# Attention queries turned in fp32, two heads at a time, with their high and low parts made from the turned bank

## What is computed

```python
aq = rope(aq.reshape(B, S, ATT_HEADS, ATT_HEAD_DIM), positions)   # 16 heads of 64
ak = rope(ak.reshape(B, S, ATT_KV_HEADS, ATT_HEAD_DIM), positions)  # 4 key heads
...
scores = jnp.einsum('bnqhgd,bnkhd->bnhgqk', qb, kk) * (hd ** -0.5)  # blocks of 128, window of two blocks
scores = jnp.where(mask, scores, -jnp.inf)
mx = jnp.maximum(scores.max(axis=-1, keepdims=True), sink)
p = jnp.exp(scores - mx)
probs = p / (p.sum(axis=-1, keepdims=True) + jnp.exp(sink - mx))
out = jnp.einsum('bnhgqk,bnkhd->bnqhgd', probs, vv)
```

## Time and profile before

| | us |
|---|---|
| median of 3 runs | 1392.05 (1391.99 to 1392.17) |
| the profiled execution | 1391.64 |
| its span, first to last instruction | 1389.9 |
| PE busy | 1328.2 (96%) |
| DVE busy | 668.1 (48%) |
| ACT busy | 397.0 (29%) |
| POOL busy | 662.6 (48%) |
| turning `q_parts` on PE, L607, x128 | 21.0 |
| `q_high` on ACT, L852, x32 | 417 to 422 ns each |

### The profile page before, as it was taken

One profiled execution on the slowest core, in us unless ns is written; L12 is line 12 of the kernel. 1 busy time (PEld: TensorE's weight loads), 2 busy tenths in 40 slices (PEclk: granted clock), 3 DMA queues, 4 the chain that ended last, 5 costly groups with the idle time before them and its releaser, 6 DMA issues.

```text
span 1389.9 us, 20009 instructions
## 1 busy us (share of the span) xinstructions
PE 1328.2 (96%) x6846; PEld 1128.8 (81%) x6846; DVE 668.1 (48%) x1297; ACT 397.0 (29%) x926; POOL 662.6 (48%) x854
## 2 busy tenths in 40 slices
PE   3499999999999999999999999999999999999997
PEld 2398797989877888889978987898789888688886
DVE  5979886785873000153265235424542321544335
ACT  5334445353450100023322332333132311311111
POOL 6834507061366544295267146715661455557340
PEclk9799999999999999999999999999999999999999
DMA  9411102010021220230131031103210132321502
GB/s 350 123 45 31 47 2 61 15 32 28 0 61 61 75 79 26 89 93 17 48 89 30 0 90 46 30 0 92 59 30 15 45 92 91 106 91 61 197 16 106
DMA packets 119832, 89.30 MB, mean 64 GB/s; under 512 B 13305, under 2 KB 111721, under 8 KB 118894
## 3 DMA queue, kind: packets, MB, share of 16 engines
q1 hardware_dynamic: 116288, 76.16, 17.9%
q10 hardware_dynamic: 3502, 12.61, 2.6%
HBM read 80.35 MB, written 8.41 MB: 64 GB/s over the span
## 4 chain that ended last, share of the span: by engine, by line
PE 82%; DVE 12%; issue 2%; ACT 2%; DVEq 0%; ACTq 0%
PE pp L532 24%; PE pp L533 23%; PE pp L534 23%; PE pp L718 2%; PE pp L728 2%; PE pp L638 1%; DVE y_lo L1294 1%; DVE prob L1237 1%; DVE num L1404 1%; PE pp L710 1%; PE pp L621 1%; PE pp L629 1%; PE pp L723 1%; PE pp L622 1%; PE pp L607 1%
## 5 line engine op out<-in xcount | busy, mean ns | idle before, releaser
L484 POOL TENSOR_TENSOR w_hi<-raw,ones 128x256 fp32r<-128x256 f32 x404 | 284.1, 734 | 619.1 <-ACTq L346 341.0
L532 PE MATMUL pp<-h_hi,w_hi 128*128 128x512 f32 x912 | 361.5, 396 | 9.9 <-DVE h_lo L1120 8.3
L533 PE MATMUL pp<-h_lo,w_hi 128*128 128x512 f32 x912 | 356.1, 390 | 0.0
L534 PE MATMUL pp<-h_hi,w_lo 128*128 128x512 f32 x912 | 355.9, 390 | 0.0
L488 POOL TENSOR_TENSOR w_lo<-raw,w_hi 128x256 fp32r<-128x256 f32 x404 | 345.7, 887 | 7.9
L532 PEld LDWEIGHTS pp<-h_hi,w_hi 128*128 128x128 f32 x912 | 171.8, 188 | 49.6 <-issue 6.8
L534 PEld LDWEIGHTS pp<-h_hi,w_lo 128*128 128x128 f32 x912 | 171.8, 188 | 36.0
L533 PEld LDWEIGHTS pp<-h_lo,w_hi 128*128 128x128 f32 x912 | 171.9, 188 | 34.6
L532 PE MATMUL pp<-w_hi,h_hi 128*128 128x384 f32 (+1 forms) x512 | 162.1, 317 | 0.6 <-DVE roped L1214 0.6
L534 PE MATMUL pp<-w_hi,h_lo 128*128 128x384 f32 (+1 forms) x512 | 158.1, 309 | 0.0
L533 PE MATMUL pp<-w_lo,h_hi 128*128 128x384 f32 (+1 forms) x512 | 158.0, 309 | 0.0
(11 more groups left out here) (216 smaller groups left out, 1855.9 us busy)
## 6 DMA issues: line engine op xcount, KB each, us to landing
raw<-w_in SPq DMA_DIRECT2D x72, 512.0 KB, 3.6
w_mod<-w_ada SPq DMA_DIRECT2D x7, 1024.0 KB, 11.5
x_in<-x SPq DMA_DIRECT2D x4, 1024.0 KB, 8.0
raw<-w_att SPq DMA_DIRECT2D x8, 512.0 KB, 5.0
merged_dram<-mix_a ACTq DMA_DIRECT2D x8, 512.0 KB, 2.6
w_gate<-w_ada ACTq DMA_DIRECT2D x8, 512.0 KB, 3.4
raw<-w_m SPq DMA_DIRECT2D x8, 512.0 KB, 3.6
mix_in<-merged_dram ACTq DMA_DIRECT2D x8, 512.0 KB, 3.3
```

The source lines that it names most:

```text
L484: ins = pool.tensor_tensor(hi[:, q, :], raw[:, s, q, :], one[:, q, :], ALU.mult)
L532: pe.matmul(o, lh, rh, start=first, stop=False)
L533: pe.matmul(o, lh, rl, start=False, stop=False)
L534: return pe.matmul(o, ll, rh, start=False, stop=last)
```

## The change

The two heads of a pair are turned together, in fp32, straight out of `roped`: a transpose of 128 tokens by 2 x 64. In bank 2 the even head of the pair then stands on partitions 0 to 63 and the odd one on 64 to 127. `copy_qk` copies each half to the same half of `q_t` as fp32r, the high part; `q_low` subtracts it from the bank and writes the low part to the other half of `q_t`. So the even heads have high above low and the odd ones low above high, which is the same to `scores`. `q_high`, `q_parts` and `ident_r` go. `q_low` moves from block u-2 to block u-3, ahead of `k_low`, and waits for `copy_qk`; `turn_q` waits until `q_low` of the block before has read the bank; `scores` waits for `q_low`.

```diff
             def turn_q(i, m):
-                after(pe, q_lo_ready, NB * i + m + 1)
                 after(pe, qk_copied, 2 * (NB * i + m))
-                for g in range(4):
-                    ins = pe.matmul(bank(2)[:, g * P:(g + 1) * P], q_parts[:, m % 2, g, :, :], ident_r[:, :], start=True, stop=True)
+                after(pe, q_lo_ready, NB * i + m)
+                for pair in range(2):
+                    ins = pe.transpose(bank(2)[:, pair * P:(pair + 1) * P], roped[:, m % 2, 2 * pair:2 * pair + 2, :, :], ident[:, :])
                 ins.then_inc(qk_turned, 1)
             def scores(i, m):
                 after(pe, qk_copied, 2 * (NB * i + m + 1))
                 after(pe, k_lo_ready, NB * i + m + 1)
+                after(pe, q_lo_ready, NB * i + m + 1)
...
-            def q_high(i, m):
-                after(act, rope_done, 2 * (NB * i + m + 1))
-                if m >= 2:
-                    after(act, qk_turned, NB * i + m - 1)
-                act.activation(q_parts[:, m % 2, :, 0, :], roped[:, m % 2, 0:4, :, :].rearrange("p h a d -> p h (a d)"), ACT.Copy).then_inc(q_hi_ready, 1)
             def copy_qk(i, m):
                 after(act, qk_turned, NB * i + m + 1)
                 after(act, scores_full, NB * i + m)
-                act.activation(q_t[:, :, :], bank(2).rearrange("p (g t) -> p g t", g=4), ACT.Copy).then_inc(qk_copied, 1)
+                for odd in range(2):
+                    r = slice(odd * HD, (odd + 1) * HD)
+                    ins = act.activation(q_t[r, odd:4:2, :], bank(2)[r, 0:2 * P].rearrange("p (g t) -> p g t", g=2), ACT.Copy)
+                ins.then_inc(qk_copied, 1)
...
             def q_low(i, m):
-                after(dve, q_hi_ready, NB * i + m + 1)
-                dve.tensor_tensor(q_parts[:, m % 2, :, 1, :], roped[:, m % 2, 0:4, :, :].rearrange("p h a d -> p h (a d)"),
-                                  q_parts[:, m % 2, :, 0, :].bitcast(F32), ALU.subtract).then_inc(q_lo_ready, 1)
+                after(dve, qk_copied, 2 * (NB * i + m + 1))
+                for odd in range(2):
+                    r, other = slice(odd * HD, (odd + 1) * HD), slice((1 - odd) * HD, (2 - odd) * HD)
+                    ins = dve.tensor_tensor(q_t[other, odd:4:2, :], bank(2)[r, 0:2 * P].rearrange("p (g t) -> p g t", g=2),
+                                            q_t[r, odd:4:2, :].bitcast(F32), ALU.subtract)
+                ins.then_inc(q_lo_ready, 1)
```

More of the change, by code:

```diff
@@ L204, in build @@
         roped = place("roped", [P, 2, 6, 2, 32], F32, X + 7168)
-        ident_r = place("ident_r", [P, P], F32R, X + 10240)
         rot_c = place("rot_c", [P, 10, 32], F32, X + 11264)
         rot_s = place("rot_s", [P, 10, 32], F32, X + 12544)
-        q_parts = place("q_parts", [P, 2, 4, 2, HD], F32R, SCR)
         q_t = place("q_t", [P, 4, P], F32R, SCR + 4096)
@@ L284, in build @@
         x_mod_act, x_mod_dve, h_hi_ready, h_lo_ready = sem("x_mod_act"), sem("x_mod_dve"), sem("h_hi_ready"), sem("h_lo_ready")
-        gates_full, gates_out, ident_r_ready = sem("gates_full"), sem("gates_out"), sem("ident_r_ready")
+        gates_full, gates_out = sem("gates_full"), sem("gates_out")
         row_step, row_act, rows_turned, cols_step = sem("row_step"), sem("row_act"), sem("rows_turned"), sem("cols_step")
@@ L290, in build @@
         rope_product, rope_done, v_copied = counter("rope_product"), counter("rope_done"), counter("v_copied")
-        q_hi_ready, q_lo_ready = counter("q_hi_ready"), counter("q_lo_ready")
+        q_lo_ready = counter("q_lo_ready")
         qk_turned, qk_copied, k_lo_ready = counter("qk_turned"), counter("qk_copied"), counter("k_lo_ready")
@@ L659, in attend @@
                         pe.wait_ge(gates_out, 4)
-                        pe.wait_ge(ident_r_ready, 1)
                     if 2 <= u <= NB + 1:
@@ L824, in _ @@
             act.wait_ge(h_lo_ready, KT)
-            act.activation(ident_r[:, :], ident[:, :], ACT.Copy).then_inc(ident_r_ready, 1)
             def gate_row_step(n):
@@ L882, in attend @@
                         exponentials(i, u - 4)
-                    if 1 <= u <= NB:
-                        q_high(i, u - 1)
                     if 9 <= u <= 12:
@@ L1257, in attend @@
                     if 3 <= u <= NB + 2:
+                        q_low(i, u - 3)
                         k_low(i, u - 3)
@@ L1260, in attend @@
                         split_window(i, u - 5)
-                    if 2 <= u <= NB + 1:
-                        q_low(i, u - 2)
                     if 4 <= u <= NB + 3:
```

## The result

| | before | after |
|---|---|---|
| median, us | 1392.11 (12 runs, 1391.73 to 1393.79) | 1395.79 (12 runs, 1394.31 to 1396.84) |
| profiled execution, us | 1391.64 | 1396.05 |
| its span, us | 1389.9 | 1394.3 |
| PE waits for `prob_t` | 2.0 us, 2 times | 5.8 us, 14 times |
| PE waits for `prob` | 1.8 us, 7 times | 3.3 us, 12 times |

The changed kernel is slower: ratio 1.0024, 95% interval 1.0016 to 1.0032. The forecast was 1396.9, with slower the likeliest. The sign and most of the total are as forecast; how the total is spread over the heads is not, so that the total is near in part by luck.

A forecast was written before the change was run, and what follows sets the result against it. PE was taken to bound the kernel, with 82% of the chain against DVE's 12%. Three heads +4.05, the first +1.5 and a single -0.75 gave +4.8 us on 1391.64; predicted median 1396.9, range 1390.5 to 1400.

The forecast's parts named there:

- PE's gain per block: On PE, six fp32 turnings replace eight: 0.20 us gained in each of 32 blocks, 6.4 if nobody waits.
- DVE's distance: On DVE, start of `sink_d` to start of `prob_t`: 1.27 us instead of 0.28, so `prob_t` comes 0.99 later.
- my case: On DVE, alternating halves hold both `q_low` operations and `k_lo`; `prob_t` 0.99 later, +4.8 us, 1396.9; chance 0.60.
- A: Rival: DVE's neighbours overlap despite alternating halves; `prob_t` 0.66 later, -0.9 us in all, 1391.1; chance 0.25.
- The new waits: In units 6 and 7 of a head, PE waits 0.22 us for `prob_t` and keeps 0.20: nothing gained.
- The table load's cover: On ACT, heads 2 to 4: 1.28 us move to the first `copy_qk`; `k_lo` of block 0 has 0.4 left.
- The chained steps 8 and 9: Units 8 and 9 of a head, bounded by DVE: two at 0.63 add 1.26 us, from 0.6 ahead to 0.7 behind.
- Step 10: Unit 10 of a head, where `q_low` is new: 0.99 us more on DVE, 0.27 and 0.10 absorbed, +0.62.
- The first head: Longer chain with gate rows on DVE and ACT's two copies in the way: -0.6 + 0.15 + 1.26 + 0.72 = +1.5 us.
- The second head: Besides the +1.35 us of each later head, PE's waits at unit 3 and for turning queries go once: -0.75.
- Rival B: DVE's additions hide entirely, as it is busy only 59 of 81 us: -6.4 - 0.75, 1384.9; chance 0.06.
- Rival C: On DVE, the `q_low` halves cost 0.6 us each start to start: 1.5 a head, 6 in all, 1403; chance 0.09.

The follow-up runs named there:

- one-sided run: The changed kernel with both `q_low` operations on partitions 0 to 63 from block 1 of each head, odd low parts left out: 1394.79 us.
- early rows: Gate rows' product and scan moved from step 9 to steps 2 and 3 of the first head: changed kernel 1390.65 us, kernel before 1388.95.
- PE's part alone: The kernel before with queries turned by two fp32 transposes of `roped` instead of four products of `q_parts`, all else left: 1387.12 us.
- slots freed late: The changed kernel with weight slots 0 to 2 signalled free in DVE's step 9 instead of at `rope` of block 7: 1395.59 us.
- low parts once: The changed kernel with `q_low`'s two operations done only for block 0 of each head, waits and order kept: 1386.22 us.
- row halves: The changed kernel with one 128x256 copy, one 128x256 `q_low`, and 12 score products over 64 rows, low by low left out: 1387.11 us.

## Why the forecast was right, and where it was not

- **PE's gain per block**: taken 0.20 (0.17 to 0.22), measured 0.22 to 0.25; in a whole head 1.17 to 1.2 when nothing hinders it. The six turnings take 0.63, under the row-made 0.66 to 0.71.
- **DVE's distance**, the step that decided between my case and A: 1.30 for 1.27, with the two `q_low` 0.44 apart. The one-sided run shows that this is the alternation (0.34 without), and how much it matters: 0.10 a block, 0.3 us in heads 2 and 3. A stood on the price of the distance, 0.33 for each `q_low` and 0.20 for `k_lo`; the one-sided run has the first and still costs 1394.79, so it tests A by half only; with `k_lo` overlapping as well nothing was run.
- **The new waits**: forecast 0.22 in steps 6 and 7, measured 0.19 and 0.18, so the gain there is nil, as said. The table load's cover held: in the third head `k_lo` is ready at 257.92 and PE wants it at 258.27, 0.35 of slack for 0.4.
- **The chained steps 8 and 9** were mis-sized: 0.97 for 1.26. PE's gain up to there (-0.72 for -0.6) is right; what failed is the term "two steps at 0.63", which held all other DVE durations fixed. They shrank. Under POOL's splits the durations depend on what POOL does at that moment. The timeline of DVE, second head, step 9, before and then after:

```profile
217.11 0.67 DVE L1232 TENSOR_TENSOR p_den<-p_sum,sink_e 128x4 f32<-128x4 f32 x1
```

```profile
220.36 0.43 DVE L1227 TENSOR_TENSOR p_den<-p_sum,sink_e 128x4 f32<-128x4 f32 x1
...
221.04 2.21 DVE L1232 TENSOR_SCALAR prob<-prob,p_rec 128x128 f32<-128x128 f32 x4
```

  `p_den` gave back 0.24 and `prob` 0.12 against the 2.33 of the earlier trace rows: 0.36, near the 0.29 missing. What `p_den` loses is what is left of POOL's operation at that moment: POOL's `w_lo` beside it ends at 217.77 and 220.78, `p_den` at 217.78 and 220.79. In before that `w_lo` is itself longer; it begins 0.01 behind the old `q_low` (216.76), which has two SBUF inputs. Timelines of POOL, before and then after:

```profile
216.77 1.00 POOL L488 TENSOR_TENSOR w_lo<-raw,w_hi 128x256 fp32r<-128x256 f32 x1
```

```profile
220.05 0.73 POOL L486 TENSOR_TENSOR w_lo<-raw,w_hi 128x256 fp32r<-128x256 f32 x1
```

  So a part of the 0.24 comes from the removal of the old `q_low`, which the forecast counted on DVE only; how large a part isn't shown.
- **Step 10**: 0.29 for 0.62, by the same cause. DVE, second head, step 10, before and then after:

```profile
223.46 0.18 DVE L1191 SCALAR_TENSOR_TENSOR neg_m<-s_max,h_neg_sink 128x4 f32<-128x4 f32 x1
223.68 0.66 DVE L1195 TENSOR_TENSOR sink_d<-neg_m,h_neg_sink 128x4 f32<-128x4 f32 x1
```

```profile
226.35 0.31 DVE L1183 SCALAR_TENSOR_TENSOR neg_m<-s_max,h_neg_sink 128x4 f32<-128x4 f32 x1
226.70 0.16 DVE L1187 TENSOR_TENSOR sink_d<-neg_m,h_neg_sink 128x4 f32<-128x4 f32 x1
```

  `sink_d` gives back 0.50, `neg_m` takes 0.13; 0.37, against the 0.33 missing. The waits for `prob` over 0.5 us that the forecast put into steps 9 and 10 did not come: step 9 has 0.34 for `prob_t` and twice 0.24 for `prob`, step 10 none. The working's own terms, -0.6 + 1.26 + 0.62, make 1.28 a head where it says 1.35 (1.32 with the 0.7 that it rounds to), 0.2 us over three heads.
- **The first head** was the wrong term of the sum: +1.5 forecast, +3.40 measured. With early rows it costs 1.17. With late ones the chain up to the first product behind the pause costs 2.03, 0.5 more than forecast, of which the `prob` of step 10 has 0.74 that the working held fixed, and the clock 1.3, which it left out: "if the clock is granted below 1.00" stood among the things to watch, but for step 3 of the later heads, and it fell in step 10 of the first, behind a pause that the trace of before already had at 1.5 us.
- **The second head**: -0.48 for +1.35 - 0.75 = +0.6. Against the third head's +0.54, what it gains once is 1.02, not 0.75. In before it was 1.04 longer than the third head (82.17, 81.13), in after 0.02: the rows to size this were in the trace, as the difference of two heads, and I had summed waits instead.
- The errors partly cancel: 1.9 too little in the first head, 1.1 too much in the second, 0.8 and 0.85 too much in the third and fourth, and 0.5 outside attention was not forecast, leaving 1396.05 for 1396.4 on the profiled execution. That the median came within 1.1 us of the forecast is luck to that extent; the sign is not, since heads 3 and 4 alone and the kernels with early rows (+1.7) show it too.
- **Rival B** (all hidden, 1384.9) is what the runs without most of `q_low` came to, 1386.22, and 1383.54 with early rows: the profile offers no cover for q_low in steps 6 to 10. **Rival C** needed 0.6 an operation and is out.

## What to carry to other kernels

Where two small operations work on the two halves of the partitions, ask whether one over all 128 can replace them: it costs DVE as much as one half, and products over 64 rows on the other half came free on TensorE here. A few tenths added to a chain that TensorE waits for can cost more elsewhere than where they are added, so look for the longest pause of TensorE in the stretch that the change touches and shorten it first. Price a recurring wait by the difference of two otherwise equal loop turns, not by the sum of its waits.

## What the runs showed of the hardware

**The clock.** The granted clock fell to 0.50 behind the first head's pause in the profiled runs of five kernels, for 3.4 us in four and for 6.8 in the one-sided run, and not there in those with early rows. The windows of PE's part alone, whose longest wait for `prob_t` is 1.5 us:

```profile
145.00:148.00 3.00, 2.78 (x11) 2.65 (x12) 3.00 (x3) 1.28 (x1) 3.00 (x3) 0.52 0.01 3
148.00:150.00 2.00, 2.00 (x9) 1.58 (x8) 1.90 (x5) 0.35 (x2) 0.43 (x1) 0.87 0.15 18
```

It fell with longest waits of 1.5 (this), 1.9 (one side) and 2.0 to 2.2 us (after, slots freed late), also in the kernel with `q_low` behind `prob_t`, whose longest was 1.0; it stayed at 1.00 with 1.3 (low parts once), 1.5 (before) and 1.6 (row halves). So the length of one wait doesn't decide it, and what does stays open. Behind attention, at about 1200 us, the traces show the same: PE has a pause of 2.2 us in all fourteen traces (2.7 in one), and the clock falls to 0.50 for 3.4 us around its end in seven of them, after among them (from 1210) and before not. It costs little there, as from the end of attention to the end of the span all take 989.3 to 989.7 us. Whether it falls may differ from one execution to the next, which would explain why most kernels with late rows scatter by 1.5 to 3.2 us and four of the five with early rows by 0.5 or less. I have one trace of each, two kernels with late rows scatter by 0.3 only, and the fifth with early rows by 2.7, so that is argued, not shown.

**POOL beside DVE.** The 4-element operations with two SBUF inputs take 0.16 alone and up to 0.68 while POOL splits weights; those that read PSUM (`q_low`, `k_lo`, `prob_t`) keep 0.42, 0.29 and 0.68 in the same steps. The Trainium skill, "SBUF — State Buffer", section "SBUF: two separate sides", says that an operation of DVE with two SBUF inputs, or in a 2-port perf mode, and one of POOL that reads SBUF lock each other out of a shared pair of ports. The rows of this case agree for two inputs: the small operations end within 0.01 to 0.02 us of POOL's `w_lo`, and the old `q_low`, 128x256 with two SBUF inputs, kept its 0.41 in step 9 while the `w_lo` begun behind it took 1.00 and not 0.73. `prob`, with one tensor from SBUF, is slowed too (2.05 for 0.88); in which mode it runs no row shows. PSUM-reading work that is put between them in steps 8 to 10 moves them to another moment of POOL's, and here that gave a part of its time back; that this was chance in the placing, not a rule, the 2.50 of `prob` with slots freed late suggests.
